# The first projection as split fp32r products, and an earlier bias in a fused attention, MoE and mLSTM kernel

## The reference, cut to what matters

```python
h = rms_norm(x, ln1_g)                      # x: 512 x 1024
z = h @ w_in                                # w_in: 1024 x 1440
q_a, k_a, v_a, c_q, c_kv, k_rope = split(z) # 512, 128, 128, 384, 256, 32 columns
q_a, k_a = rms_norm per head of 64
s = q_a k_a^T / 8 + rel_bias[t5_bucket(rel)]   # 8 heads, 2 kv heads, blocks of 128 rows x up to 384 keys
p = softmax([s, sink]); o_a = p v_a
o_b = latent_attention(c_q, c_kv, k_rope, w_qb, w_kvb, ...)
x = x + [norm(o_a), norm(o_b)] @ w_o
x = x + expert_choice_ffn(rms_norm(x), w_router, w_gate, w_up, w_down)
...
mod = silu(c) @ w_mod + b_mod               # w_mod: 1024 x 6144, for c and c_ctx
```

## Time and profile before

| | |
|---|---|
| median of 3 runs | 1682.54 us (1679.12 to 1687.13) |
| profiled execution, own time | 1681.47 us |
| its span | 1679.7 us |
| TensorE busy (matmul) | 1532.8 us, 91% of the span |
| TensorE weight loads busy | 977.8 us, 58% |
| DVE / ACT / POOL busy | 594.3 / 465.8 / 116.3 us |
| read from HBM | 300.07 MB, 181 GB/s over the span |
| mean granted clock of TensorE | 0.957 |
| chain that ended last, by engine | PE 69%, DMA 17%, DVE 6%, ACT 3% |

### The profile page before, as it was taken

How to read it: one execution, slowest core, us unless ns; L and a number is a source line. 1 busy time by engine, 2 the same in 40 slices (tenths; PEclk the granted TensorE clock), 3 DMA queues, 4 the chain that set the end, 5 groups by cost and what they waited for, 6 DMA issues and landing times.

```text
span 1679.7 us, 17716 instructions
## 1 busy us (share of the span) xinstructions
PE 1532.8 (91%) x7240; PEld 977.8 (58%) x7240; DVE 594.3 (35%) x1102; ACT 465.8 (28%) x857; POOL 116.3 (7%) x126
## 2 busy tenths in 40 slices
PE   7958949999499999999997799998989999999998
PEld 3434525655343344333332589995668788888886
DVE  0144364434512222211222632205465533243334
ACT  2143335532100110001011511217652433212322
POOL 2000033000000000000000300000020311001100
PEclk9988988999699999999999799998899999999999
DMA  5279440030499999999998021213012232222221
GB/s 211 29 223 392 163 163 0 1 138 0 171 418 421 421 421 421 422 422 420 421 421 323 1 75 57 71 54 123 1 38 69 82 100 100 87 87 83 95 76 50
DMA packets 80898, 305.40 MB, mean 182 GB/s; under 512 B 7053, under 2 KB 43174, under 8 KB 54195
## 3 DMA queue, kind: packets, MB, share of 16 engines
q1 hardware_dynamic: 80136, 304.14, 46.9%
q0 software_dynamic: 512, 0.09, 0.1%
q10 hardware_dynamic: 170, 0.05, 0.0%
HBM read 300.07 MB, written 4.19 MB: 181 GB/s over the span
## 4 chain that ended last, share of the span: by engine, by line
PE 69%; DMA 17%; DVE 6%; ACT 3%; POOL 2%; SPq 1%; issue 1%; ACTq 0%; DVEq 0%; POOLq 0%
PE ps L719 11%; PE ps L762 11%; PE ps L763 11%; PE ps L764 11%; DMA sb<-in_w_gate 7%; DMA sb<-in_w_up 5%; PE ps L612 3%; DMA bias_rows_dram<-sb 3%; PE ps L844 2%; PE ps L441 2%; PE ps L567 2%; PE ps L559 2%; DMA sb<-in_w_down 2%; PE ps L671 1%; PE ps L592 1%
## 5 line engine op out<-in xcount | busy, mean ns | idle before, releaser
L719 PE MATMUL ps<-sb 128*64 128x512 f32 x1536 | 352.4, 599 | 16.4 <-DMA sb<-in_w_gate 5.9
L719 PEld LDWEIGHTS ps<-sb 128*64 128x64 f32 x1536 | 103.0, 136 | 222.8 <-issue 178.3
L981 ACT ACTIVATE sb<-ps 128x512 f32<-128x512 f32 (+3 forms) x216 | 102.0, 483 | 423.4 <-PE ps L671 101.0
L762 PE MATMUL ps<-r_act,r_top 128*128 128x512 f32 x352 | 138.8, 394 | 3.5 <-POOL r_act L2007 2.3
L764 PE MATMUL ps<-r_act,r_low 128*128 128x512 f32 x352 | 138.4, 393 | 0.0
L1878 DVE TENSOR_TENSOR r_low<-raw,r_top 128x2048 fp32r<-128x2048 f32 x33 | 74.4, 2296 | 80.1 <-ACT r_top L981 80.1
L1673 DVE TENSOR_TENSOR sb<-sb,ps 128x512 f32<-128x512 f32 x64 | 43.8, 687 | 141.3 <-PE ps L708 141.2
L763 PE MATMUL ps<-r_low,r_mid 128*128 128x512 f32 x240 | 93.4, 389 | 0.0
L762 PE MATMUL ps<-r_low,r_h 128*128 128x256 f32 x320 | 90.7, 283 | 0.0
L763 PE MATMUL ps<-r_low,r_h 128*128 128x256 f32 x320 | 90.6, 283 | 0.0
L764 PE MATMUL ps<-r_low,r_top 128*128 128x256 f32 x288 | 81.5, 283 | 0.0
(11 more groups left out here) (364 smaller groups left out, 2454.0 us busy)
## 6 DMA issues: line engine op xcount, KB each, us to landing
sb<-in_w_gate SPq DMA_DIRECT2D x64, 1024.0 KB, 25.9
sb<-in_w_up SPq DMA_DIRECT2D x64, 1024.0 KB, 26.0
sb<-in_w_down SPq DMA_DIRECT2D x64, 1024.0 KB, 26.5
sb<-in_w_mod SPq DMA_DIRECT2D x16, 1536.0 KB, 9.7
raw<-in_f_w_up SPq DMA_DIRECT2D x22, 1024.0 KB, 7.6
raw<-in_a_w_in SPq DMA_DIRECT2D x12, 1024.0 KB, 5.3
raw<-in_f_w_down SPq DMA_DIRECT2D x5, 2048.0 KB, 8.1
sb<-in_w_in SPq DMA_DIRECT2D x4, 1440.0 KB, 10.7
```

Source lines behind the costliest of these rows:

```text
L719: mm = pe.matmul(PS[64 * hf:64 * hf + 64, b * HALF:(b + 1) * HALF], lhsT(k), ring[c % RINGN][:, kk, hf * HALF:(hf + 1) * HALF], start=(k = ...
L762: pe.matmul(o, a_hi, b_hi, start=first, stop=False)
L981: return act_(o, i_, ACT.Identity, bias=bias, scale=scale)
```

## The change

1. **Projection.** x turned and scaled is rounded to `xT_hi` by ACT for all k; w_in likewise to `w_in_hi`. DVE computes `xT_lo` and `w_in_lo`, the latter in w_in's own place. `xT_lo` lies in x's place. TensorE makes three fp32r products in place of one fp32 product. `zsq` gets four places of its own.
2. **Bias.** The one-hot and mask table is cut to its 32 used rows and loaded with the bias table ahead of x; the bias product stands ahead of x's transposes; ACT issues the write of the bias rows after its rounding loop.
3. **Loads.** `w_in_hi` lies over the places of w_qb, w_kvb and part of w_o. w_qb, w_kvb and w_router are loaded behind slice 6 of w_mod, w_o behind slice 15.
4. **Scores.** `kz` has two tiles in place of four: kv head g stands in both halves of the partitions, and a score product contracts the 64 partitions of its head. Nothing is cleared.
5. **Modulation.** Turn b of the window makes the products of k = b-1 for b = 1 to 7; only k = 7 follows the latent projections.

```diff
@@ tensor
+            pe.wait_ge(*at("hot_in"))
+            pe.wait_ge(*at("relb_in"))
+            claim(1, ("bvec", 0))
+            pe.matmul(PS[0:AH, HALF:2 * HALF], relb[0:32, :], hot[0:32, :], start=True, stop=True).then_inc(*inc("pe_bvec"))
...
-                        claim(k, ("xT_" + "da"[k % 2], k))
+                        claim(k, ("xT_l", k))
...
-                        pe.wait_ge(*at("xT_" + "da"[k % 2], k))
-                        if k % 2 == 0:
-                            pe.wait_ge(*at(f"w_in{k // 2}"))
+                        pe.wait_ge(*at("xT_l", k))
+                        pe.wait_ge(*at("wi_l", k))
...
-                            mm = pe.matmul(bank(bank_of["z", t, c], ZCH), xT[:, k, t * P:(t + 1) * P],
-                                           w_in[:, k, c * ZCH:(c + 1) * ZCH], start=(k == 0), stop=(k == KD - 1))
+                            tok, col = slice(t * P, (t + 1) * P), slice(c * ZCH, (c + 1) * ZCH)
+                            mm = split_product(bank(bank_of["z", t, c], ZCH), xT_hi[k][:, tok], xT_lo[k][:, tok],
+                                               w_in_hi[:, k, col], w_in_lo[:, k, col], k == 0, k == KD - 1)
...
-                    pe.matmul(bank(x, (hi - lo + 1) * P), qTa[:, h // 2, n * P:(n + 1) * P],
-                              kz[:, 2 * g + h % 2, lo * P:(hi + 1) * P], start=True, stop=True).then_inc(*inc("pe_As", (b, i)))
+                    r = slice(64 * (h % 2), 64 * (h % 2) + 64)
+                    pe.matmul(bank(x, (hi - lo + 1) * P), qTa[r, h // 2, n * P:(n + 1) * P],
+                              kz[r, g, lo * P:(hi + 1) * P], start=True, stop=True).then_inc(*inc("pe_As", (b, i)))
...
-                if b < 6:
-                    mod_rows(b)
+                if b:
+                    mod_rows(b - 1)
...
-            mod_rows(6)
             mod_rows(7)
@@ scalar
-            for k in range(1, KD, 2):
+            for k in range(KD):
                 eng.wait_ge(*at("pe_xT", k))
-                copy(xT[:, k, :], bank(k), scale=col1[:, C_LN1 + k:C_LN1 + k + 1]).then_inc(*inc("xT_a", k))
+                copy(xT_hi[k][:, :], bank(k), scale=col1[:, C_LN1 + k:C_LN1 + k + 1]).then_inc(*inc("xT_h", k))
+                if k % 2 == 0:
+                    eng.wait_ge(*at(f"w_in{k // 2}"))
+                copy(w_in_hi[:, k, :], w_in[:, k, :]).then_inc(*inc("wi_h", k))
+            eng.wait_ge(*at("bvec"))
+            eng.dma_start(bvec_dram, bvec[0:AH, :].unsqueeze(1).broadcast_to([AH, P, S])).then_inc(*inc("bvec_out", 0, 16))
@@ vector
+            eng.wait_ge(*at("pe_bvec"))
+            ve.tensor_tensor(bvec[0:AH, :], bank(1)[0:AH, :], outside[0:AH, :], ALU.add).then_inc(*inc("bvec"))
...
+            for k in range(KD):
+                eng.wait_ge(*at("xT_h", k))
+                ve.scalar_tensor_tensor(xT_lo[k][:, :], bank(k), col1[:, C_LN1 + k:C_LN1 + k + 1], xT_hi[k][:, :].bitcast(F32),
+                                        ALU.mult, ALU.subtract).then_inc(*inc("xT_l", k))
+                eng.wait_ge(*at("wi_h", k))
+                ve.tensor_tensor(w_in_lo[:, k, :], w_in[:, k, :], w_in_hi[:, k, :].bitcast(F32), ALU.subtract).then_inc(*inc("wi_l", k))
@@ gpsimd
-            eng.memset(kz, 0.0).then_inc(*inc("kz0"))
@@ sync
+            sp.dma_start(modrow[0:32, 0:2, :].rearrange("p a b -> p (a b)"), I["const_b"][0:32, :]).then_inc(*inc("hot_in", 0, 16))
+            sp.dma_start(relb[0:32, :], I["rel_bias"]).then_inc(*inc("relb_in", 0, 16))
...
-            sp.dma_start(modrow[:, 0:2, :].rearrange("p a b -> p (a b)"), I["const_b"]).then_inc(*inc("hot_in", 0, 16))
-            sp.dma_start(relb[0:32, :], I["rel_bias"]).then_inc(*inc("relb_in", 0, 16))
-
-            sp.wait_ge(*at("bvec"))
-            sp.dma_start(bvec_dram, bvec[0:AH, :].unsqueeze(1).broadcast_to([AH, P, S])).then_inc(*inc("bvec_out", 0, 16))
             sp.wait_ge(*at("bvec_out"))
...
                 sp.dma_start(w_mod[:, m % 3, :], wm[:, m // 2, (m % 2) * 3072:(m % 2 + 1) * 3072]).then_inc(*inc(f"w_mod{m % 3}", m, 16))
+                if m == 6:
+                    sp.wait_ge(*at("st"))
+                    sp.dma_start(w_qb, I["w_qb"].rearrange("a (k p) n -> p (a k) n", p=P)).then_inc(*inc("w_qb", 0, 16))
+                    sp.dma_start(w_kvb, I["w_kvb"].rearrange("a (k p) n -> p (a k) n", p=P)).then_inc(*inc("w_kvb", 0, 16))
+                    sp.dma_start(wr, I["w_router"].rearrange("a (k p) n -> p (a k) n", p=P)).then_inc(*inc("wr_in", 0, 16))
+            sp.dma_start(w_o, I["w_o"].rearrange("a (k p) n -> p (a k) n", p=P)).then_inc(*inc("w_o", 0, 16))
```

More of the change, by code:

```diff
@@ L56 @@
 SHARED = {
-    "pe_front": "pe_vec pe_vec2 pe_bvec pe_xT pe_z pe_T",
+    "pe_front": "pe_vec pe_bvec pe_vec2 pe_xT pe_z pe_T",
     "pe_window": "pe_As pe_At pe_Ao pe_mod",
@@ L237, in program @@
         hot, outside, bvec = modrow[:, 0, :], modrow[:, 1, :], modrow[:, 2, :]
-        w_in = sb(W_IN, KD, 1440)
+        w_in, w_in_lo, w_in_hi = (view(v[:, 0:KD * 1440], KD) for v in (RAW, R_LOW, R_MID))
         w_qb = sb(W_QB, 3, 768)
@@ L245, in program @@
         x_res = sb(XR, NT, D)
-        xT = sb(T16, KD, S)
+        xT_hi = [place(f"r_xhi{k}", T16 + k * S, S, F32R) for k in range(KD)]
+        xT_lo = [place(f"r_xlo{k}", XR + k * S, S, F32R) for k in range(KD)]
         junk = sb(QKV + 7168, D)
-        zsq = sb(XR, NT, QKW)
+        zsq = [sb(o, QKW) for o in (W_IN + 11520, 12288 + 11520, SPARE, SPARE + QKW)]
         zqk = sb(Z, NT, QKW)
@@ L252, in program @@
         qTa = sb(QKV, 4, S)
-        kz = sb(QKV + 2048, 4, S)
+        kz = sb(QKV + 2048, 2, S)
         bias = sb(QKV + 4096, AH, 384)
@@ L404, in nb, with split_product @@
                 return b
+            def split_product(o, a_hi, a_lo, b_hi, b_lo, first, last):
+                pe.matmul(o, a_hi, b_hi, start=first, stop=False)
+                pe.matmul(o, a_hi, b_lo, start=False, stop=False)
+                return pe.matmul(o, a_lo, b_hi, start=False, stop=last)
             pe.wait_ge(*at("const_in"))
@@ L758, in _ @@
             turn[0] = 0
-            def split_product(o, a_hi, a_lo, b_hi, b_lo, first, last):
-                pe.matmul(o, a_hi, b_hi, start=first, stop=False)
-                pe.matmul(o, a_hi, b_lo, start=False, stop=False)
-                return pe.matmul(o, a_lo, b_hi, start=False, stop=last)
             for k in range(KD):
@@ L1024, in _ @@
                 eng.wait_ge(*(at("zsq", t - 1) if t else at("ssq1", 3)))
-                act_(zsq[:, t, :], zqk[:, t, :], ACT.Square, scale=AD ** -0.5)
+                act_(zsq[t], zqk[:, t, :], ACT.Square, scale=AD ** -0.5)
                 act_(junk[:, 0:CQ], zr[:, t, 128:512], ACT.Square, scale=CQ ** -0.5, accum_out=st[:, t, 10:11])
@@ L1040, in _ @@
             eng.wait_ge(*at("pe_T", 4))
-            eng.wait_ge(*at("kz0"))
             for n in range(4):
                 g, e = divmod(n, 2)
-                copy(kz[64 * e:64 * e + 64, n, :], bank(bank_of["T", 4])[64 * g:64 * g + 64, :],
+                copy(kz[64 * e:64 * e + 64, g, :], bank(bank_of["T", 4])[64 * g:64 * g + 64, :],
                      scale=col2[64 * g:64 * g + 64, C_AK:C_AK + 1]).then_inc(*inc("kz", n))
@@ L1398, in _ @@
             ve.tensor_copy(col1, bank(0, P)).then_inc(*inc("cols"))
+            eng.wait_ge(*at("pe_bvec"))
+            ve.tensor_tensor(bvec[0:AH, :], bank(1)[0:AH, :], outside[0:AH, :], ALU.add).then_inc(*inc("bvec"))
             eng.wait_ge(*at("cols"))
-            for k in range(0, KD, 2):
-                eng.wait_ge(*at("pe_xT", k))
-                ve.tensor_scalar(xT[:, k, :], bank(k), col1[:, C_LN1 + k:C_LN1 + k + 1], None, ALU.mult).then_inc(*inc("xT_d", k))
             eng.wait_ge(*at("ssq1", 3))
+            eng.wait_ge(*at("pe_xT", KD - 1))
+            for k in range(KD):
[4 more added lines that the diff above has]
+                ve.tensor_tensor(w_in_lo[:, k, :], w_in[:, k, :], w_in_hi[:, k, :].bitcast(F32), ALU.subtract).then_inc(*inc("wi_l", k))
             mean_eps(rs[:, 0:4], ssq[:, 0:4], D).then_inc(*inc("rs1e"))
@@ L1411, in _ @@
                     ve.tensor_copy(col2, bank(bank_of["vec2"], P)).then_inc(*inc("cols2"))
-                    eng.wait_ge(*at("pe_bvec"))
-                    ve.tensor_tensor(bvec[0:AH, :], bank(bank_of["bvec"])[0:AH, :], outside[0:AH, :], ALU.add).then_inc(*inc("bvec"))
                     eng.wait_ge(*at("cols2"))
@@ L2022, in _ @@
                 sp.dma_start(w_in[:, 2 * j:2 * j + 2, :], wv[:, 2 * j:2 * j + 2, :]).then_inc(*inc(f"w_in{j}", 0, 16))
-            sp.dma_start(modrow[:, 0:2, :].rearrange("p a b -> p (a b)"), I["const_b"]).then_inc(*inc("hot_in", 0, 16))
-            sp.dma_start(relb[0:32, :], I["rel_bias"]).then_inc(*inc("relb_in", 0, 16))
-            sp.wait_ge(*at("bvec"))
-            sp.dma_start(bvec_dram, bvec[0:AH, :].unsqueeze(1).broadcast_to([AH, P, S])).then_inc(*inc("bvec_out", 0, 16))
             sp.wait_ge(*at("bvec_out"))
```

(4 more changed lines are left out.)

10 lines of the change are left out of this document (3 added, 7 removed).

## The result

The changed kernel takes 1675.35 us (median of 6 runs, 1672.29 to 1677.51), the kernel before 1685.49 (6 runs, 1679.12 to 1687.13): a ratio of 0.9945, 95% interval 0.9925 to 0.9965. That is 10.1 us, or 0.6%, faster. The forecast was 1663.5 from a base of 1682.54, a gain of 19, and its range ended at 1674. The sign came out, the size didn't: about half of the gain, and the time is 1.4 us outside the range. Of the 11.9 us between forecast and time, 2.9 are the base: the six runs of the kernel before have a median that is 2.9 higher than the three that the forecast had.

A forecast was written before the change was run, and what follows sets the result against it. The expert weight stream was taken to bound the kernel, passing front savings on one for one. Projection 4.0 and the window gave 18.9 us off, 1662.6 profiled, 1663.5 as median; range 1655 to 1674.

The forecast's parts named there:

- What bounds the kernel: Whole kernel: the expert weight stream, issued from 420.06 us, bounds it; front savings by then return one for one.
- The projection: First projection: three fp32r products per fp32 product end it at 92.8 in place of 96.8, saving 4.0 us.
- Evacuation to the first scores: Between projection and first scores: same operations, 14.4 us as before, so first scores at 107.2; gain 0.
- The bias: Bias write: issued at 34, over at 78, rows loaded by 86, first used at 108; modulation weights start at 92.8.
- rival b: Bias write decides again: at twice its time, slices start at 122 and the kernel takes 1679; chance 0.05.
- The window stage: First scores to latent projections: 64.8 us in place of 79.7, ending at 172.0, paced by modulation weight loads.
- first modulation product at 116.8 ... slice 3 streams from 120.6: Window start: the first modulation product frees its slot at 118.2; slice 3 of w_mod streams from 120.6.
- 3.84 us: Window's w_mod stream: each 1536 KB slice takes 3.84 us at 410 GB/s; slices 3 to 13 take 42.2.
- Its product 1.4 and the last transposes and values 2.2: Window's end: TensorE work after slice 13 lands at 168.4, ending the stage at 172.0.
- (a): Window's w_mod slices come slower, 363 GB/s or 4.33 us each: stage end 178.3, kernel 1670; chance 0.12.
- (c): Input splits cost 1.5 times the price: k=0 hangs until 38, scores 5.5 later, kernel 1669; chance 0.05.
- (d): TensorE held at its low clock long after k=0; through the whole projection, the kernel ends at 1720; chance 0.03.

The follow-up runs named there:

- the fillers: Changed kernel plus products of no use in two TensorE waits, 24 before the first T transposes and 9 before the first turn's transposes; 1673.81 us.
- the second profile: Profile of the changed kernel run once more without any edit; median 1677.23 us, profiled span 1672.3, stage end 181.4.
- four buffers: Changed kernel with w_qb, w_kvb, w_router and w_o loaded behind slice 2 and a fourth buffer for w_mod; 1661.59 us.

## Why the prediction was right or wrong

**What bounds the kernel:** right. The rest behind chunk 8 is 1259.6 us before and 1260.4 after. From the stage end to chunk 8 it is 229.2 us before and 230.6 after, so the second half of "one for one" lost 1.4. The chain shows the loss at the start of the products with w_o, first after the change, then before it:

```profile
353.63 4.12 PE ps L584 x32
357.75 16.55 PE ps L619 x32
```

```profile
361.76 3.47 PE ps L577 x32
365.23 13.84 PE ps L612 x32
```

The same instructions take 3.4 us more, and the granted clock from 300 to 420 us is 0.96 where it was 1.00; the rest of that way was 2 us shorter. Why the clock fell there is open. The forecast had nothing for it. The profiled execution is 14.9 us over the 1662.6 that the forecast had for one like the profile of before: 12.7 at the stage end, 1.4 from there to chunk 8, 0.8 behind it.

**The projection:** right, 3.2 for 4.0, with its mechanism: first product 22.84 for 21.8, the last four of six groups 2.23 apart for 2.31. The early bias product, counted as nothing, is the likely 1 us at the start: ScalarE's first rounding began at 19.07, held 0.66 by x's transposes, where 18.1 was forecast. At half clock a product of three took 1.2 us where VectorE gave one each 2.23, so most of the low clock there was hidden.

**Evacuation to the first scores:** 93.6 to 108.84 is 15.2 for 14.4. Listed durations of the T transposes (5.52 before, 6.76 after) hold the difference; with the fillers the same 37 take 4.26. Before:

```profile
104.65 5.52 PE L455 MATMUL ps<-sb 128*128 128x128 f32 x37 [0.26 <-DVE sb L1439]
```

The step "Same operations ... 14.4" overlooked that a duration comes with a clock.

**The bias:** right that it no longer decides (rival b fell). What the part is worth by itself was not asked, and is 1 to 3 us.

**The window stage: this is the step that failed.** It was priced at 64.8 and took 75.8 (72.6 in the second profile). Mechanism, places and order were right: w_mod's stream sets the end, TensorE waits at slice 7 and before slice 13. Its terms were too small, and all on one side:

- "first modulation product at 116.8 ... slice 3 streams from 120.6": 121.1, and 124 in the windows. The transposes and the first turn at 1.2 GHz are the whole of it, since fillers bring the first product to 116.58. Some 3.5 us.
- "3.84 us" a slice: the busy windows moved 379, 395 and 401 GB/s, not 410. The 11 slices and the other loads are 19.6 MB (47.8 us at 410): 50 at the mean of 392, 2.2 more.
- a stream without a gap: between 162 and 166 it moved 131 GB/s, a third of its pace for 4 us, so 2.7 lost. By the order of the buffers slice 11 waits there for the products of slice 8, which the late slice 7 had pushed to 161.6. The second profile has 312 there, and its stage ends 3.3 sooner.
- "Its product 1.4 and the last transposes and values 2.2": 178.94 to 184.67 is 5.7, for 3.6. The product behind the wait took 3.49 at 1.2 GHz; even at 2.4 it would have been 1.91. 2.1 more.

3.5 + 2.2 + 2.7 + 2.1 is 10.5 of the 12.7 that the stage end was late by; the rest was not taken apart. w_qb, w_kvb and w_router behind slice 6 were in the sum with 5.6, so they are no part of the error; they are the part of the change that gives its gain away, which the forecast priced and didn't remark on.

**The rivals:** (a), slower slices, 1670 at 363 GB/s, was right in kind; it priced 6.3 us at the stage end, where pace and gap together came to 4.9. (c), dearer splits, fell with 2.23 for 2.31. (d), the low clock through the projection, didn't come: it lasted to 35 us. The starts 0.40 apart end there. But the low clock did come in small pieces wherever TensorE waited for some us, and no rival had that. The Trainium skill's figure for loads from HBM (DMA: Bandwidth & Descriptors, Where 436 GB/s comes from), about 358 GB/s, did not bind here, where one core runs: 427 GB/s over 16 us with four buffers. The Trainium skill's "Up to 2×" for a contraction of 64 (TensorEngine Tiling (Array Packing), Theoretical Speedup) nearly came: 2.78 to 1.49 between starts.

**The range** took four terms at their likeliest value, and gave each error a case of its own. They fell together, and a stage without slack passes each of them on. Had two been let run together (the start 3.5 later, and 363 GB/s), the stage end would have been 178.3 + 3.5 = 181.8 and the time 1673.3 before any spread of the runs, and with that spread the range would have gone past 1675.

## What to carry to other kernels

Before a load is put into a stream, look for the stretch in which the stream stands still for want of a buffer, and put it there: 2.3 MB moved by four slices gave 6.6 to 8.4 us, and one more buffer, once w_o was moved too, some 6.6 again. A long item of the chain is worth only what the next one leaves: the 44 us write, taken off, gave 1 to 3. Where a stage is paced by a queue, sum its terms at their bad ends together as well, and price what TensorE does behind a wait of several microseconds at 1.2 GHz.

## What the runs showed of the hardware

- TensorE's clock behind waits for w_mod. In the profiles of the changed kernel and its variants the 12 products behind a wait of 4.5 us or more took 3.2 to 3.6 us, those behind one of up to 1.9 took 1.91; in between (2.2 to 3.8) both occurred. Filler products in the waits behind the projection kept the granted clock from 95 to 108 us at 1.00, for 0.61.
- Two fp32 score products on the upper and lower 64 rows run at once: 8 of 384 columns in 1.49 us between starts, for 2.78 over full height.
- An fp32r product of 480 columns stands 0.22 us from the next at 2.4 GHz and 0.40 at 1.2.
- The issue of w_o took 0.43 us behind slice 15, and 10.0 to 11.0 directly behind slices 0 to 2 and the small weights (four runs). The issuing queue itself stood still so long, with all behind it. In the kernel before, the issue of w_router, behind the bias rows, w_qb, w_kvb and w_o, took 7.69.
- The write of the bias rows, 2 MB of copies of 8 rows, moved some 49 GB/s while it ran (28 to 70 us), and took 43.6 to 44.7 us; in the windows with loads of w_mod at full stretch it was 379 to 427.
- ScalarE's queue issued the bias write at 27.71, while it still had three of its eight rounds of roundings to do, though the write stands behind them in its program. How far ahead a queue can get no run shows.
